# Weight sums of the feed-forward stage made once, during the mLSTM stage, and read back from DRAM

## The chip, the cores and the metric

The kernel runs on one core of one Trainium2 chip. The metric is the device time of one execution in microseconds (us). TensorE (PE) multiplies, VectorE (DVE), ScalarE (ACT) and GpSimd (POOL) work elementwise, SyncE (SP) issues nearly all DMAs. Each engine takes its instructions in the order in which they are written, and waits on semaphores.

## The reference

One layer of a hybrid decoder for a prompt of 2048 tokens and 64 sample tokens. The change touches how the matrix `w_ffn_in` is prepared; the sum itself stays.

```python
h = rms_norm(x, norm_mix_w)
... attention heads and mLSTM heads on h @ w_in ...
x = x + jnp.concatenate([o_att, o_ml], axis=-1) @ w_out
h2 = rms_norm(x, norm_ffn_w)
g, u = jnp.split(h2 @ w_ffn_in, 2, axis=-1)          # w_ffn_in: 1024 x 5632
gp = jnp.concatenate([conv_buf, g], axis=1)
gc = conv_b + gp[:, 0:T] * conv_w[0] + gp[:, 1:T+1] * conv_w[1] + gp[:, 2:T+2] * conv_w[2]
x = x + (jax.nn.silu(gc) * u) @ w_down
```

## The kernel before

All data are float32. To keep precision, each matrix product is made as three: an operand is rounded on ACT (`_hi`), the rest is subtracted on DVE (`_lo`), and PE adds hi times hi, lo times hi and hi times lo.

The stages follow each other: attention (0 to about 300 us), mLSTM (`mlstm`, to about 670 us), then `late`: the output projection with the second norm (the loop over `positions`, to about 890 us), the feed-forward rounds (to about 1930 us) and the down projection in 77 turns (to the end).

**The mLSTM stage** goes through 17 tiles, one each period; tile 14 is the sample tokens. In a period PE projects the next tile (`project(t + 1, g)`, three groups), and does the recurrence of this one in between (`turn`, `scores`, `sums`). POOL does `keep_v` and `weigh_k` at the start of a period and `square_h` near its end, once DVE's `divide` has made h; `rstd_h` and `weigh_h` then alternate with DVE's `norm_out`, `scale_out` and `finish_out`, which stand in DVE's queue ahead of `make_a` of the next tile, for which PE's `sums` waits. SP loads the tile after next (`load_h`), the row of gates (`load_m`), and stores the last output (`store_o`).

**The feed-forward rounds.** There are three groups of columns of h2 (group 0: 512 prompt tokens and the 64 sample tokens; groups 1 and 2: 768 each). Each group goes through 11 rounds, `r = (G, i)`; a round takes 256 columns of the gate half of `w_ffn_in` (unit u = 0) and 256 of the up half (u = 1). The 2 by 2 block product of a unit is made by seven products of half the size, in Strassen's manner (Winograd's form), `PRODUCTS`. With B11, B21 (left half of the columns) and B12, B22 (right half; top and bottom rows) the seven right-hand sides are B11, B21, B22 and the sums T1 = B12 - B11, T2 = B22 - T1, T3 = B22 - B12, T4 = B21 - T2. A product is 4 chunks of 3 matmuls; 14 products, 168 matmuls, make a round. Group 0 adds `sample_down`, 12 matmuls for the sample tokens.

The weights of a unit come in one DMA of 1 MiB (`load_b`, L2551) into `c_raw[u]`. POOL makes the four sums (`sums_b`, L3372 to L3385): T1 in place in `c_raw`, T2 to T4 in `t_raw[u]`. ACT rounds four pieces (`round_b`): q = 0 is B11, B21, q = 1 is T1, B22, q = 2 is T2, q = 3 is T3, T4. DVE subtracts them (`split_b`) in the same order, and PE's products wait on `b_split`. `t_raw` and `t_lo` are the same memory, so a new sum there waits until PE has used the old one (`w_prod(pool, before(r), 7 * u + 6)`). Since every group needs the same weights, the sums are made three times over the kernel.

SP's order in a round r is: `load_b(0, after(r))`, in group 0 `load_d(before(r))`, `store_act(before(r))` (L2558), `load_b(1, after(r))`. `store_act` holds two waits: for POOL's gates (`w_made`, L2565), and for DVE's sums of the last activations (`w_sums`, L2568). `load_b(1, ...)` stands behind both. At a group's last round `load_next_a` follows: seven DMAs of up to 768 KiB bring the left-hand sides of the next group.

POOL's order in a round (`step`, L3420): `sums_b(r, 1)`, the two gates of the round before, `heads`, `tails`, `sums_b(after(r), 0)`.

## Time and profile before

| | us |
|---|---|
| median of 3 runs | 2361.06 (2360.82 to 2361.8) |
| the profiled execution, its own time | 2364.47 |
| its span, first to last instruction | 2362.7 |
| PE busy | 2253.2 (95%) |
| DVE busy | 1620.8 (69%) |
| POOL busy | 1034.6 (44%) |
| ACT busy | 899.3 (38%) |
| DMA moved | 333.95 MB, mean 141 GB/s |

The rounds of the feed-forward stage take some 1040 of the 2363 us. A share of busy time is a mean over stages that differ: the views by stretch and the chain of waits tell which engine a stage waits for. Matmuls overlap in the profile, so their rate is read from the distance of their starts and not from their durations.

### The profile page before, as it was taken

The numbers are of one execution on the slowest core, as the hardware profiler recorded it, in microseconds if no ns is written. First come the engines' busy times: TensorE is split into PE (matmuls) and PEld (weight loads), VectorE is DVE, ScalarE is ACT, GpSimd is POOL, SyncE is SP. The second block draws the span as 40 slices with busy tenths as digits, with TensorE's granted clock in tenths as the row PEclk, the third lists the DMA queues.
The fourth block names the chain that finished last, engine by engine and source line by source line (L and its number), as shares of the span: only waits on it lengthen the run. The fifth ranks groups of instructions, "written<-read, shape, count | busy, mean of one in ns | idle before, by whom it ended". The sixth has DMA issues, their size and how long they took to land.

```text
span 2362.7 us, 34413 instructions
## 1 busy us (share of the span) xinstructions
PE 2253.2 (95%) x13423; PEld 1984.9 (84%) x13423; DVE 1620.8 (69%) x2271; ACT 899.3 (38%) x1524; POOL 1034.6 (44%) x811
## 2 busy tenths in 40 slices
PE   7999999999999998888879999989999999999999
PEld 6899878887777888777768999988999998888887
DVE  5666655556573457888878899888998974445653
ACT  4555622222232324444444444444444433233331
POOL 4333312222121346655554666655666630245730
PEclk9999999999999998999998999999999999999999
DMA  8433222222154553444344333353333345686454
GB/s 283 151 126 121 79 86 81 81 81 67 45 183 142 192 184 122 156 139 138 132 161 140 117 118 116 118 181 100 119 118 119 119 158 190 219 289 202 139 177 165
DMA packets 208076, 333.95 MB, mean 141 GB/s; under 512 B 23083, under 2 KB 148679, under 8 KB 205847
## 3 DMA queue, kind: packets, MB, share of 16 engines
q1 hardware_dynamic: 207883, 331.69, 41.5%
q8 instruction: 107, 1.75, 0.3%
q14 instruction: 54, 0.44, 0.1%
q0 software_dynamic: 32, 0.07, 0.0%
HBM read 235.42 MB, written 97.24 MB: 141 GB/s over the span
## 4 chain that ended last, share of the span: by engine, by line
PE 65%; DVE 7%; DMA 5%; issue 4%; POOL 3%; ACT 3%; SPq 0%; DVEq 0%; POOLq 0%; ACTq 0%
PE bank L114 12%; PE bank L115 12%; PE bank L116 12%; PE bank L2803 9%; PE bank L2804 8%; PE bank L2805 8%; DMA late_c_raw<-in_w_ffn_in_dram 3%; DVE late_t L3184 1%; DVE late_s_act L3154 1%; DVE late_t_lo L3129 1%; POOL late_c_raw L3381 1%; POOL late_t_raw L3385 1%; DVE late_t L3187 1%; DMA late_a_raw<-h_parts 1%; ACT late_t_hi L2930 1%
## 5 line engine op out<-in xcount | busy, mean ns | idle before, releaser
L2803 PE MATMUL bank<-late_a_hi,late_b_hi 128*128 128x384 f32 (+1 forms) x1056 | 350.0, 331 | 56.3 <-issue 18.6
L2804 PE MATMUL bank<-late_a_lo,late_b_hi 128*128 128x384 f32 (+1 forms) x1056 | 344.7, 326 | 0.0
L2805 PE MATMUL bank<-late_a_hi,late_b_lo 128*128 128x384 f32 (+1 forms) x1056 | 343.2, 325 | 0.0
L2803 PE MATMUL bank<-late_a_hi,late_t_hi 128*128 128x384 f32 (+1 forms) x792 | 262.9, 332 | 19.6 <-DVE late_gp L3172 8.5
L2803 PEld LDWEIGHTS bank<-late_a_hi,late_b_hi 128*128 128x128 f32 x1056 | 201.7, 191 | 69.1 <-issue 36.3
L2804 PE MATMUL bank<-late_a_lo,late_t_hi 128*128 128x384 f32 (+1 forms) x792 | 258.3, 326 | 0.0
L2805 PE MATMUL bank<-late_a_hi,late_t_lo 128*128 128x384 f32 (+1 forms) x792 | 257.6, 325 | 0.0
L114 PE MATMUL bank<-late_e_hi,late_y_a_hi 128*128 128x512 f32 x616 | 242.1, 393 | 2.1 <-DVE late_e_lo L3202 2.1
L116 PE MATMUL bank<-late_e_hi,late_y_a_lo 128*128 128x512 f32 x616 | 242.6, 394 | 0.0
L115 PE MATMUL bank<-late_e_lo,late_y_a_hi 128*128 128x512 f32 x616 | 241.7, 392 | 0.0
L3379 POOL TENSOR_TENSOR late_t_raw<-late_c_raw 128x512 f32<-128x512 f32 x64 | 84.2, 1315 | 327.9 <-DMA late_c_raw<-in_w_ffn_in_dram 300.4
L3129 DVE TENSOR_TENSOR late_t_lo<-late_t_raw,late_t_hi 128x512 fp32r<-128x512 f32 (+1 forms) x132 | 220.8, 1672 | 10.0 <-POOL late_t_raw L3385 10.0
L3129 DVE TENSOR_TENSOR late_b_lo<-late_c_raw,late_b_hi 128x1024 fp32r<-128x1024 f32 x128 | 187.3, 1463 | 46.6 <-ACT late_b_hi L2930 46.6
L3200 DVE TENSOR_TENSOR late_y_a_lo<-late_y_a_raw,late_y_a_hi 128x1024 fp32r<-128x1024 f32 x77 | 111.4, 1447 | 154.6 <-ACT late_y_a_hi L2989 154.6
L2804 PEld LDWEIGHTS bank<-late_a_lo,late_b_hi 128*128 128x128 f32 x1056 | 201.9, 191 | 0.0
L2805 PEld LDWEIGHTS bank<-late_a_hi,late_b_lo 128*128 128x128 f32 x1056 | 201.6, 191 | 0.0
L2803 PEld LDWEIGHTS bank<-late_a_hi,late_t_hi 128*128 128x128 f32 x792 | 150.0, 189 | 32.6 <-issue 16.7
L2930 ACT ACTIVATE late_b_hi<-late_c_raw 128x1024 fp32r<-128x1024 f32 x128 | 134.9, 1054 | 94.7 <-POOL late_c_raw L3381 62.1
L3184 DVE SCALAR_TENSOR_TENSOR late_t<-late_gp,late_cc,late_t 128x768 f32<-128x768 f32 (+1 forms) x132 | 163.2, 1237 | 0.4
L114 PE MATMUL bank<-att_next_hi,att_next_hh 128*128 128x512 f32 (+1 forms) x384 | 159.9, 416 | 2.1 <-DVE ml_vx L1941 2.1
L115 PE MATMUL bank<-ahead_ml_w_lo,att_next_hh 128*128 128x512 f32 (+1 forms) x384 | 154.1, 401 | 0.0
L116 PE MATMUL bank<-att_next_hi,att_next_hh 128*128 128x512 f32 (+1 forms) x384 | 153.1, 399 | 0.0
(380 smaller groups left out, 5187.1 us busy)
## 6 DMA issues: line engine op xcount, KB each, us to landing
late_c_raw<-in_w_ffn_in_dram SPq DMA_DIRECT2D x64, 1024.0 KB, 5.1
late_y_a_raw<-act_parts SPq DMA_DIRECT2D x77, 512.0 KB, 3.6
late_e_raw<-in_w_down_dram SPq DMA_DIRECT2D x77, 256.0 KB, 4.1
act_parts<-late_s_act SPq DMA_DIRECT2D x22, 768.0 KB, 4.4
att_next_hh<-h_parts SPq DMA_DIRECT2D x16, 1024.0 KB, 4.8
late_d_raw<-in_w_down_dram SPq DMA_DIRECT2D x11, 1024.0 KB, 7.6
late_a_raw<-h_parts SPq DMA_DIRECT2D x14, 768.0 KB, 12.7
act_parts<-late_t SPq DMA_DIRECT2D x22, 384.0 KB, 2.5
```

The lines of the kernel that those rows point to most:

```text
L114: nc.tensor.matmul(out, a_hi, b_hi, start=first, stop=False)
L115: nc.tensor.matmul(out, a_hi, b_lo, start=False, stop=False)
L116: return nc.tensor.matmul(out, a_lo, b_hi, start=False, stop=last)
L2803: nc.tensor.matmul(out, w_h, hi[:, c, :], start=first, stop=False, skip_group_check=True)
L2804: nc.tensor.matmul(out, w_h, lo[:, c, :], start=False, stop=False, skip_group_check=True)
L2805: ins_ = nc.tensor.matmul(out, w_l, hi[:, c, :], start=False, stop=last, skip_group_check=True)
L2930: nc.scalar.activation(hi, raw, ACT.Copy).then_inc(b_rounded, 1)
L3129: nc.vector.tensor_tensor(lo, raw, hi.bitcast(F32), ALU.subtract).then_inc(b_split, 1)
L3154: nc.vector.tensor_tensor(out, x, y, op).then_inc(act_summed, 1)
L3184: ins_ = nc.vector.scalar_tensor_tensor(tb, gp[:, x, HEAD - s:HEAD - s + G.pn], col, tb, ALU.mult, ALU.add)
L3200: nc.vector.tensor_tensor(y_lo[s][:, :], y_raw[s][:, :], y_hi[s][:, :].bitcast(F32), ALU.subtract).then_inc(y_split, 1)
L3379: nc.gpsimd.tensor_tensor(tt(T3), b(1, 1), b(0, 1), ALU.subtract).then_inc(b_summed, 1)
```

## The change

Four parts.

1. **Sums ahead.** A class `SumsAhead` makes T1 to T4 of all 22 units (11 rounds, two halves) during mLSTM tiles 2 to 12 and puts them into a DRAM tensor `weight_sums`. A tile handles four items; an item is half a unit (two chunks of the top rows and the two of the bottom rows under them). For an item SP loads 2 times 256 KiB, POOL makes 4 subtractions of 128x256 elements, and SP stores 256 + 3 times 128 KiB in four DMAs (B11 and T1 as one image, T3, T4, T2). POOL does them between `weigh_k` and `square_h`, 16 subtractions in a tile. SP stores a tile's items one period later, in pairs, and loads the next into the same buffers as soon as the stores of that item have landed. The buffers lie over memory that is free then. `wait_all` stands on ACT, DVE and POOL ahead of the sample tile and on SP in `late`.
2. **Rounds load them.** `load_b` becomes two DMAs of 512 KiB: B11 and T1 from `weight_sums`, B21 and B22 from `w_ffn_in`. A new `load_t` loads the 768 KiB of T3, T4, T2 into `t_raw[u]` when PE has done the last T product of the unit of the round before. `sums_b` and the waits on it are gone from POOL, ACT and DVE.
3. **SP's order in a round** is now `load_t(1, r)`, `load_b(0, after(r))`, `load_d`, `store_act(before(r))`, `load_b(1, after(r))`, `load_t(0, after(r))`, `store_sums(before(r))`: the store of the activations' sums, with its wait on DVE, has left `store_act`.
4. In the down projection the two semaphores of a turn's two loads become one (`ye_in`), so ACT and POOL wait for both.

```diff
@@ mlstm, SP's period @@
+                for pair in range(2):
+                    if SUM_FROM < t.c <= SUM_TO:
+                        ahead.store(sp, t.c - 1, 2 * pair)
+                        ahead.store(sp, t.c - 1, 2 * pair + 1)
+                    if SUM_FROM <= t.c < SUM_TO:
+                        ahead.load(sp, ins, t.c, 2 * pair)
+                        ahead.load(sp, ins, t.c, 2 * pair + 1)
                 if 1 <= t.c <= samp.c:
                     store_o(sp, t - 1)
...
@@ mlstm, POOL's period @@
                 weigh_k(t)
+                if SUM_FROM <= t.c < SUM_TO:
+                    ahead.make(pool, t.c, 0)
+                    ahead.make(pool, t.c, 1)
+                if is_sample(t):
+                    ahead.wait_all(pool)
                 square_h(pool, t)
...
+    def load(self, sp, ins, slot, n):
+        unit, e = self.item(slot, n)
+        i, u = unit // 2, unit % 2
+        if slot > SUM_FROM:
+            sp.wait_ge(self.moved[n], self.moves(slot))
...
+    def make(self, pool, slot, pair):
+        nc = self.nc
+        two = (2 * pair, 2 * pair + 1)
+        for n in two:
+            pool.wait_ge(self.moved[n], self.moves(slot) + 32)
+            nc.gpsimd.tensor_tensor(self.diff[n], self.low[n][:, :, 1, :], self.top[n][:, :, 1, :], ALU.subtract).then_inc(self.made, 1)
...
+    def store(self, sp, slot, n):
+        unit, e = self.item(slot, n)
+        sp.wait_ge(self.made, self.count(slot, n, 3))
...
@@ late, SP @@
-            sp.dma_start(raw_of(r, u)[:, :].rearrange("p (c n) -> p c n", c=KC), src).then_inc(b_in[u], 16)
+            sp.dma_start(raw_of(r, u)[:, 0:IMAGE], sums_dram[2 * i + u, :, 0:IMAGE]).then_inc(b_in[u], 16)
+            sp.dma_start(raw_of(r, u)[:, IMAGE:2 * IMAGE].rearrange("p (c n) -> p c n", c=KH), src).then_inc(b_in[u], 16)
+
+        def load_t(u, r):
+
+            if r is None:
+                return
+            w_prod(sp, before(r), 7 * u + 5)
+            sp.dma_start(t_raw[u][:, :], sums_dram[2 * r[1] + u, :, IMAGE:IMAGE + 3 * KH * P]).then_inc(t_in[u], 16)
...
                 if r != FIRST:
+                    load_t(1, r)
                     load_b(0, after(r))
...
                     store_act(before(r))
                     load_b(1, after(r))
+                    load_t(0, after(r))
+                    store_sums(before(r))
...
@@ late, ACT's round_b @@
-                act.wait_ge(b_in[u], 16 * (turn(r) + 1))
-            else:
-                w_summed(act, r, 4 * u + q)
+                act.wait_ge(b_in[u], 32 * (turn(r) + 1))
+            elif q == 2:
+                act.wait_ge(t_in[u], 16 * (turn(r) + 1))
...
@@ late, POOL's step @@
             p = before(r)
-            if p is None:
-                heads(r)
-            sums_b(r, 1)
             if p is not None:
                 gate(p, 0)
                 gate(p, 1)
-                heads(r)
+            heads(r)
             tails(r)
-            sums_b(after(r), 0)
```

**Where instructions stand.** POOL in one round of group 0, before. `late_t<-late_t,late_up` are the gates, the copies are `heads` and `tails`, L3379 to L3385 are the sums of one unit.

```order
L3393 TENSOR_TENSOR late_t_7680<-late_t_7680,late_up 128x576 x2
L3398 COPY late_cc<-conv_cols 128x40
L3400 MEMSET late_gp 128x2x2
L3405 COPY late_gs<-late_cc 128x16x2
L3413 COPY late_gs<-late_gp 128x16x8
L3414 COPY late_s_act<-late_gp 128x32
L3417 COPY halo<-late_gp 128x4
L3379 TENSOR_TENSOR late_t_raw<-late_c_raw_7675 128x512
L3381 TENSOR_TENSOR late_c_raw_7675<-late_c_raw_7675 128x4x128
L3383 TENSOR_TENSOR late_t_raw<-late_c_raw_7675 128x512
L3385 TENSOR_TENSOR late_t_raw<-late_c_raw_7675,late_t_raw 128x512
L3379 TENSOR_TENSOR late_t_raw<-late_c_raw_7676 128x512
```

POOL in the same round now:

```order
L3494 TENSOR_TENSOR late_t_8401<-late_t_8401,late_up 128x576 x2
L3499 COPY late_cc<-conv_cols 128x40
L3501 MEMSET late_gp 128x2x2
L3506 COPY late_gs<-late_cc 128x16x2
L3514 COPY late_gs<-late_gp 128x16x8
L3515 COPY late_s_act<-late_gp 128x32
L3518 COPY halo<-late_gp 128x4
```

The eight subtractions of a round are gone; the gates follow the last round's copies at once.

SP in one round of group 0, before, from `load_b(0)` on; `late_c_raw` with its two numbers are the buffers of u = 0 and u = 1, `late_d_raw` is the down weight, and `act_parts` takes activations:

```order
L2551 DMA late_c_raw_7675<-in_w_ffn_in_dram 128x8x256
L2555 DMA late_d_raw<-in_w_down_dram 128x2x1024
L2566 DMA act_parts<-late_t_7679 128x2x256
L2567 DMA act_parts<-late_t_7679 128x256
L2569 DMA act_parts<-late_s_act 128x4x256
L2551 DMA late_c_raw_7676<-in_w_ffn_in_dram 128x8x256
```

SP in one round of group 0 now, from `load_t(1)` on (`weight_sums` is the new tensor):

```order
L2655 DMA late_t_raw<-weight_sums 128x1536
L2647 DMA late_c_raw_8396<-weight_sums 128x1024
L2648 DMA late_c_raw_8396<-in_w_ffn_in_dram 128x4x256
L2659 DMA late_d_raw<-in_w_down_dram 128x2x1024
L2670 DMA act_parts<-late_t_8400 128x2x256
L2671 DMA act_parts<-late_t_8400 128x256
L2647 DMA late_c_raw_8397<-weight_sums 128x1024
L2648 DMA late_c_raw_8397<-in_w_ffn_in_dram 128x4x256
L2655 DMA late_t_raw<-weight_sums 128x1536
L2681 DMA act_parts<-late_s_act 128x4x256
```

The load of the second unit's weights stood behind the store from `late_s_act` (DVE's sums) and now stands ahead of it; two loads of `late_t_raw` are new.

POOL in one mLSTM tile, before (`ml_vx` and `ml_kw` are `keep_v` and `weigh_k`, L1488 is `square_h`):

```order
L2115 TENSOR_TENSOR ml_vx<-att_next_z,ones 128x4x128
L2123 TENSOR_TENSOR ml_kw<-att_next_z,att_next_cols 128x256
L1488 TENSOR_TENSOR ml_hq<-ml_h 128x512
L1494 TENSOR_TENSOR ml_hr<-ml_hvar,mhalf 128x4
L1499 TENSOR_TENSOR ml_hq<-ml_h,ml_norm 128x512
```

POOL in an mLSTM tile now, to the first two of the second pair of items (six more follow ahead of `square_h`); pieces 0, 1 and 3 have buffers of their own, piece 2 uses the memory of `norm_mix` and `mask`:

```order
L2125 TENSOR_TENSOR ml_vx<-att_next_z,ones 128x4x128
L2133 TENSOR_TENSOR ml_kw<-att_next_z,att_next_cols 128x256
L2306 TENSOR_TENSOR ml_piece_diff_4301<-ml_piece0b,ml_piece0a 128x256
L2306 TENSOR_TENSOR ml_piece_diff_4302<-ml_piece1b,ml_piece1a 128x256
L2310 TENSOR_TENSOR ml_piece0a<-ml_piece0a 128x2x128
L2310 TENSOR_TENSOR ml_piece1a<-ml_piece1a 128x2x128
L2314 TENSOR_TENSOR ml_piece0b<-ml_piece0b,ml_piece0a 128x2x128
L2314 TENSOR_TENSOR ml_piece1b<-ml_piece1b,ml_piece1a 128x2x128
L2318 TENSOR_TENSOR ml_piece0b<-ml_piece0b 128x2x128
L2318 TENSOR_TENSOR ml_piece1b<-ml_piece1b 128x2x128
L2306 TENSOR_TENSOR mask<-norm_mix 128x256
L2306 TENSOR_TENSOR ml_piece_diff_4303<-ml_piece3b,ml_piece3a 128x256
```

Sixteen subtractions stand between `weigh_k` and `square_h`.

SP in two mLSTM periods, before:

```order
L1518 DMA att_next_hh<-h_parts 128x2048
L1507 DMA ml_neg_m<-gate_rows 128x512
L1436 DMA mixed<-ml_o 128x512
L1518 DMA att_next_hh<-h_parts 128x2048
L1507 DMA ml_neg_m<-gate_rows 128x512
```

SP in one mLSTM period now, first half: the stores of items 0 and 1 of the tile before, and their loads for this tile:

```order
L1519 DMA att_next_hh<-h_parts 128x2048
L1508 DMA ml_neg_m<-gate_rows 128x512
L2324 DMA weight_sums<-ml_piece0a 128x512
L2326 DMA weight_sums<-ml_piece_diff_4301 128x256
L2328 DMA weight_sums<-ml_piece0b 128x2x128 x2
L2324 DMA weight_sums<-ml_piece1a 128x512
L2326 DMA weight_sums<-ml_piece_diff_4302 128x256
L2328 DMA weight_sums<-ml_piece1b 128x2x128 x2
L2295 DMA ml_piece0a<-in_w_ffn_in_dram 128x2x256
L2295 DMA ml_piece0b<-in_w_ffn_in_dram 128x2x256
L2295 DMA ml_piece1a<-in_w_ffn_in_dram 128x2x256
L2295 DMA ml_piece1b<-in_w_ffn_in_dram 128x2x256
```

A second half of the same kind, for items 2 and 3, follows ahead of the store from `ml_o`: 24 DMAs are added to the three of a period.

## Rows read from the trace of the kernel before

**Rows 1.** Busy time by stretch: mLSTM, group 0's rounds, group 1's rounds; first line: columns.

```profile
core 0: us, PE busy (x) PEld busy (x) DVE busy (x) ACT busy (x) POOL busy (x), PEclk, DMA share, GB/s
...
330.00:600.00 270.00, 270.00 (x1395) 216.36 (x1393) 161.44 (x291) 60.52 (x148) 72.87 (x65) 1.00 0.21 75
...
918.00:1225.00 307.00, 268.68 (x1786) 241.87 (x1787) 255.92 (x326) 137.02 (x190) 186.67 (x159) 0.98 0.38 128
...
1255.00:1572.00 317.00, 315.31 (x1767) 310.41 (x1766) 282.37 (x277) 131.27 (x169) 197.72 (x134) 0.99 0.35 114
```

**Rows 2.** Chain that ended last, one round of group 0: start, us, what.

```profile
1040.97 0.36 SPq L2569
...
1041.38 6.10 DMA late_c_raw<-in_w_ffn_in_dram
...
1047.61 1.35 POOL late_t_raw L3379
...
1049.03 2.17 POOL late_c_raw L3381
...
1057.09 1.32 DVE late_t_lo L3129
...
1068.81 1.05 ACT late_d_hi L2936
...
1071.81 0.36 SPq L2569
```

**Rows 3.** Timeline of PE, group 0: start, us, engine line op names shape.

```profile
1040.33 0.45 PE L114 MATMUL bank<-late_d_hi,late_acts_hi 128*64 128x512 f32 x1
...
1043.98 0.40 PE L2803 MATMUL bank<-late_a_hi,late_b_hi 128*128 128x288 f32 x1 [0.66 <-DVE late_b_lo L3129]
1044.22 0.30 PE L2804 MATMUL bank<-late_a_lo,late_b_hi 128*128 128x288 f32 x1
...
1045.54 0.29 PE L2805 MATMUL bank<-late_a_hi,late_b_lo 128*128 128x288 f32 x1
```

**Rows 4.** DVE by line and form, group 0's rounds: count, busy us, mean ns, idle before.

```profile
L3154 DVE TENSOR_TENSOR late_s_act<-late_t 128x256 f32<-128x256 f32 x19 | 18.2, 960 | 0.0
L3154 DVE TENSOR_TENSOR late_s_act<-late_s_act,late_t 128x256 f32<-128x256 f32 x10 | 13.3, 1328 | 1.0
L3154 DVE TENSOR_TENSOR late_s_act<-late_t,late_s_act 128x256 f32<-128x256 f32 x9 | 3.8, 419 | 0.0
```

**Rows 5.** Change from group 0 to 1: chain, then PE; last line group 1 to 2.

```profile
1227.25 7.70 DMA late_a_raw<-h_parts
...
1238.66 0.66 PE L2803 MATMUL bank<-late_a_hi,late_b_hi 128*128 128x384 f32 x1 [10.15 <-issue]
...
1590.70 0.66 PE L2803 MATMUL bank<-late_a_hi,late_b_hi 128*128 128x384 f32 x1 [8.42 <-issue]
```

**Rows 6.** Timelines of one mLSTM period: POOL, DVE, PE, SP; in brackets idle and releaser.

```profile
442.01 1.04 POOL L1488 TENSOR_TENSOR ml_hq<-ml_h 128x512 f32<-128x512 f32 x1 [12.44 <-DVE ml_h L1450]
...
448.42 1.07 POOL L2123 TENSOR_TENSOR ml_kw<-att_next_z,att_next_cols 128x256 f32<-128x256 f32 x1
...
451.37 0.76 DVE L1919 TENSOR_TENSOR ml_a<-bank,ml_e 128x256 f32<-128x256 f32 x2 [2.35 <-PE bank L1614]
...
457.35 1.06 PE L1626 MATMUL bank<-ml_vx,ml_a 128*128 128x129 f32 x8
...
437.32 0.32 SPq L1518 DMA_DIRECT2D att_next_hh<-h_parts  x1
...
457.54 0.32 SPq L1518 DMA_DIRECT2D att_next_hh<-h_parts  x1
```

**Rows 7.** POOL by line and form, whole span: prices of elementwise operations.

```profile
L2115 POOL TENSOR_TENSOR ml_vx<-att_next_z,ones 128x512 f32<-128x512 f32 x16 | 20.5, 1282 | 34.0 <-DVE ml_vx L1941 30.0 <-PE bank L1630 4.0
...
L1238 POOL TENSOR_TENSOR att_v<-att_z,ones 128x128 f32<-128x128 f32 x16 | 7.4, 460 | 0.0
```

**Rows 8.** DMA queue over 1300 to 1400 us: packets, MB, share of 16 engines.

```profile
q1 hardware_dynamic: 9613, 11.39, 35.5%
```

More of the change, by code:

```diff
@@ L1285, in _, with mlstm @@
             tiles_each(period, 0, NT)
-def mlstm(nc, block, k, C, bank, ins, outs, h_dram, o_dram, start, first):
+def mlstm(nc, block, k, C, bank, ins, outs, h_dram, o_dram, start, first, ahead):
     QM, KM, VM, OM = 0, MLQ, 2 * MLQ, 2 * MLQ + MLV
@@ L1850, in period @@
                 if is_sample(t):
+                    ahead.wait_all(act)
                     forget_s()
@@ L2074, in period @@
                 if is_sample(t):
+                    ahead.wait_all(dve)
                     gates_s()
@@ L2241, in half_tile, with late @@
     return (G.base + h * G.PH) // P + j - G.tiles[0]
-def late(nc, block, k, first, bank, ident, mhalf, ins, outs, o_dram, x1_dram, h2_dram, a_dram, conv_cols, halo, ml_end):
+def late(nc, block, k, first, bank, ident, mhalf, ins, outs, o_dram, x1_dram, h2_dram, a_dram, sums_dram, conv_cols, halo, ml_end, ahead):
     CC = SB * (CW - 1) + CW + 1
@@ L2567, in store_act, with store_sums @@
             sp.dma_start(a_dram[2, i, :, cols], act_part(r, 1, 1)).then_inc(landed, 16)
+        def store_sums(r):
+            if r is None:
+                return
+            G, i = r
+            cols = slice(G.half_col(), G.half_col() + G.PH)
+            landed = act_out[turn(r) % 2]
             w_sums(sp, r, 3)
@@ L2672, in _ @@
             if p.c == SAMPLE_AT + 1:
+                ahead.wait_all(sp)
                 load_b(0, FIRST)
+                load_t(0, FIRST)
             if p is final:
@@ L2678, in _ @@
                 proj.wait(sp, final)
+                load_t(1, FIRST)
                 load_d(FIRST)
@@ L2685, in _ @@
         load_b(1, after(FIRST))
+        load_t(0, after(FIRST))
         for G in groups:
@@ L3550, in trunk_step @@
         with nc.Block() as block:
[L3551 removed]
+            ml_end = mlstm(nc, block, ml_stage, C, bank, ins, outs, h_dram, o_dram, start, first, made_ahead)
             inner.close()
```

116 lines of the change are left out of this document (75 added, 41 removed).

## The prediction

> **What bounds the kernel now.** I read the busy time by stretch first, then the chain of waits inside one feed-forward round, then the timelines of the engines in the places that the change touches.
>
> By stretch [rows 1] three cases stand apart. In the mLSTM stage PE is busy all 270.00 of 270 us: PE bounds it, and POOL works 72.87 of 270 us. In group 1's rounds PE is busy 315.31 of 317 us although DVE is at 282.37: PE bounds these too, and group 2's are of the same shape. Only in group 0's rounds does PE have gaps: 268.68 of 307 us.
>
> The chain of group 0 [rows 2] shows why. It repeats every 1071.81 - 1040.97 = 30.84 us: SP's store of the activation sums (L2569), then the load of the second unit's weights which is queued behind it (6.10 us), then POOL's sums (1.35, 2.17 and two more), ACT, DVE's `late_t_lo`, PE's next unit and DVE's work on it, and at last DVE's activation sums, which release the store again. PE itself needs less: its matmuls start (1045.54 - 1044.22) / 10 = 0.132 us apart [rows 3], 168 of them are 22.2 us; `sample_down` takes 1043.98 - 1040.33 less the wait of 0.66, 3.0 us. That is 25.2 us, 5.6 below the period.
>
> **The change, part by part.** The sum is made against the profiled span of 2362.7 us. The profiled execution took 2364.47, 3.4 more than the median of 2361.06; I take the difference of the sum off the median.
>
> *Group 0's rounds.* Two links of the chain go. `load_b(1)` no longer stands behind the wait on DVE's sums; it waits for DVE's split of the same buffer, about the middle of the round, so it is issued some 12 us earlier (`late_t_lo` at 1057.09 against 1071.81). And POOL's four subtractions between the load and ACT are gone, about 7 us (from 1047.61 to before 1054.8: ACT and DVE follow, DVE at 1057.09) [rows 2]. In their place `late_t_raw` is loaded by `load_t`. Its buffer is free about 1.6 us before the unit's end (one product of 12 matmuls at 0.132); for u = 1 `sample_down` (3.0) passes, and the second T product of the next round is a whole unit (11 us) later. A load of 1 MiB took 6.10 us, this one is 768 KiB: it is hidden with some 7 us to spare. For u = 0 likewise.
>
> DVE gets lighter too. Its second activation sum (`late_s_act<-late_s_act,late_t`, 128x256) takes 1328 ns while POOL makes sums, and the last one, of the same size with POOL idle, 419 ns; the mean of the other two is 960 [rows 4]. These alone are 0.91 + 2 x 0.54 = 2.0 us of a round. The Trainium skill ("SBUF — State Buffer", Who interferes with whom) says the same of the cause: a DVE instruction with two SBUF inputs and a GpSimd instruction that reads SBUF lock each other out for a whole instruction. What it adds here comes with the mLSTM stage.
>
> What is late next: the tail of DVE's queue in a round. The second silu, ACT's `round_d` (1.05 us at 1068.81), DVE's split of it, two activation sums, two taps and three splits stand ahead of PE's second product of the next round; this chain doesn't run over POOL, and PE waited 0.66 us at its head even now [rows 3]. Also POOL's gates now run right where DVE makes those splits, and can cost one blocked instruction. From below the round is 25.2 us plus restarts of a few tenths: 26.0. From above, if a gate blocks one split and each product waits once, 28.0. I take 26.9, nearer to the floor, because PE in group 1 keeps its rate [rows 1] with DVE busy for 89% of the time, and here DVE would have at most (255.92 / 307 x 30.84 - 2.0) = 23.7 of 26.9 us, 88%. The gain is 11 x (30.84 - 26.9) = 43 us; bounds 11 x 2.8 = 31 and 11 x 4.8 = 53.
>
> *Groups 1 and 2.* PE already has no gaps within the rounds, so nothing is gained, and DMA traffic grows from 114 GB/s [rows 1] by 1.5 MiB a round of some 29 us, 54 GB/s, far from full. 0 us; bounds +1 and -3.
>
> *Changes of group.* PE stands still 10.15 us and 8.42 us [rows 5]. The left-hand sides were queued behind `store_act` with DVE's sums and behind the 1 MiB of `load_b(1)`; that load is now out of the way. A MB costs 35.5 us / 11.39 = 3.1 us of the queue [rows 8], and DVE's sums come about 1 us sooner, so both changes shrink by about 4 us: 8 us. The first load took 7.70 us [rows 5], so it can't be much more; bounds 3 and 12.
>
> *The mLSTM stage* pays. The period is 457.54 - 437.32 = 20.2 us. POOL's own work runs from 442.01 to 448.42 + 1.07, 7.5 us, and leaves 12.7 free [rows 6]. A subtraction of 256 elements lies between 460 ns (128) and 1282 ns (512) [rows 7]; on the line between, 0.73 us, plus 0.07 from one to the next (1047.61 + 1.35 to 1049.03) [rows 2]: 16 x 0.80 = 12.9 us. So POOL is full: `square_h` comes at least 0.2 us later in each of 11 tiles, and with about 1 us of blocked instructions 1.2 us, 13 in all. This has slack: DVE idles 2.35 us ahead of `make_a`, and PE's `sums` start at 457.35, 5.2 us after `make_a` has ended [rows 6], 7.6 us together. Beyond that PE waits: some 6 us.
>
> By the lock of the page above, each of DVE's two-input instructions in this stretch (the gate caps, the division) may be held for up to a whole subtraction; with three held in the division the tail would come 2 us later per tile and the stage would lose about 20 us instead. No row of before shows such a pair here.
>
> DMA is nearly full too: 75 GB/s [rows 1] x 20.2 us are 1.5 MB, the new moves 4 x (512 + 640) KiB are 4.7 MB, and 6.2 MB x 3.1 us are 19.3 of 20.2 us [rows 8]. SP waits twice a tile for stores to land before it may load; while it does, the queue still holds the other item's stores, so I expect a rate just below what is needed, and add 3 us. Total -9 us; bounds 0 (the line's price, no conflicts) and -30 (a tile of 23.5 us).
>
> *The rest.* In the down projection a turn's rounding waits for two loads instead of one. PE is fed from a ring of four turns, so 0. The waits ahead of the sample tile are for stores issued a period earlier: 0.
>
> The sum: 43 + 0 + 8 - 9 = 42 us less, a span of 2321; against the median 2361.06 - 42 = 2319 us.
>
> **The rivals.**
>
> *A. Group 0 stays bound by its chain.* DVE's tail, lengthened by POOL's gates, could hold the round at 29 us or more. For it: PE's waits in the round are on DVE. Against it: two links of 6 and 7 us leave the cycle. Gain 11 x 1.8 = 20, plus 5, less 9: 2345.
>
> *B. The mLSTM stage goes over to DMA and POOL.* A tile takes 23.5 us instead of 20.2: 11 x 3.3 = 36, less the slack of 7.6: 29 us lost instead of 9. For it: the two loads on the DMA queue and POOL computed above, both over 95%. Result 2339. It is inside my range.
>
> *C. Slower than before: SP's queue becomes the bound of the mLSTM stage.* 27 DMAs stand in a tile, each about 0.4 us of SP's time (0.32 for `load_h` [rows 6]), 11 us; four times SP waits until a store has landed. At 2 us each this fits (19 us); if stores land after 5 us, since they queue behind 6 MB, a tile is 11 + 4 x 4 = 27 us, `load_h` stands behind it, and PE gets its tile late: 11 x 6.8 - 8 = 67 us lost, against 51 gained: 2377. It decides from 25.3 us a tile.
>
> *D. The change doesn't do what it says:* the T loads land late, because they can't be issued before PE has used the old ones, and group 0 waits for them as it did for the sums, groups 1 and 2 begin to. Against it are the 7 us to spare. About 2360.
>
> **How the numbers follow.** Forecast (rounds of 26 to 28, a stage that loses 0 to 20): 0.68. A 0.11, B 0.10, C 0.07, D 0.04. The forecast alone spans 2361 - 53 - 12 = 2296 to 2361 - 31 - 3 + 20 = 2347; since its ends need all at once, 2302 to 2340. With A and B inside and half of the faster corner, the range is 2298 to 2346, which leaves out C, D and about 0.08 at the edges. What a measurement of this kernel can tell from no change is about 0.2%, 4.7 us. Faster by more: 0.68 + 0.11 + 0.10 = 0.89, less a little for B going further: 0.88. Within: 0.04, most of D. Slower: C and the rest, 0.08.
>
> **What would show it.** Right: rounds of group 0 of 26 to 28 us; `late_s_act` at 0.42 us in all four; ACT's rounding of `late_t_hi` not waiting for DMA; the first load of `late_a_raw` before the end of PE's round, and a PE gap below 7 us there; POOL's idle time in mLSTM near zero in tiles 2 to 12, PE's waits there below 20 us in all. Wrong: ACT waiting for DMA in `late_t_hi` (D); PE idle ahead of L1626 of more than 2 us a tile (B), or ahead of the projection, waiting for `att_next_hh` (C); PE's waits in group 0 on DVE's `late_b_lo` growing (A).

## The result and the profile after

The changed kernel takes 2370.35 us (median of six, 2366.43 to 2372.82), the kernel before 2361.61 beside it: ratio 1.0034, interval 1.0024 to 1.0045. It is slower by 0.34%, where 1.8% faster was forecast. The profiled execution took 2366.69 us, near the low end of the six; before's took 2364.47. One execution of one experiment took 7511 us and is left out of every number below.

Where the 2.2 us between the two profiled executions come from, by the starts of PE's rounds:

| stretch | before | after | difference | forecast |
|---|---|---|---|---|
| to the first feed-forward product | 887.1 | 897.3 | +10.2 | +9 |
| ten rounds of group 0 | 311.3 | 294.2 | -17.0 | -39 (of -43 for eleven) |
| last round before, first after each change of group | 163.6 | 151.9 | -11.7 | -12 (-8, and -4 for the eleventh round of group 0) |
| rounds 2 to 10 of groups 1 and 2, with group 2's last | 569.4 | 589.5 | +20.1 | 0 |
| down projection | 431.3 | 431.9 | +0.6 | 0 |

Forecast and profile lie 44 us apart: 22 of them in group 0's rounds, 20 in those of groups 1 and 2.

Busy time by stretch after, to be read beside [rows 1] (the same columns):

```profile
330.00:600.00 270.00, 262.59 (x1330) 208.55 (x1329) 173.70 (x281) 58.77 (x142) 194.57 (x234) 1.00 0.80 258
918.00:1225.00 307.00, 272.01 (x1853) 252.76 (x1851) 229.08 (x342) 135.01 (x195) 57.95 (x80) 0.98 0.58 191
1255.00:1572.00 317.00, 307.88 (x1728) 301.14 (x1728) 226.68 (x267) 126.89 (x165) 60.07 (x50) 1.00 0.49 163
```

POOL has nearly nothing left to do in the rounds (197.72 to 60.07 us in group 1), DVE is lighter by 56 us there, and yet PE, which had no gaps in group 1, has them now: 307.88 of 317. A lighter DVE and a slower PE together say that something got worse at one place of the round, not in the sum.

That DVE got lighter is as forecast. DVE by form in group 0's rounds (count, busy us, mean ns), against [rows 4]:

```profile
L3245 DVE TENSOR_TENSOR late_b_lo<-late_c_raw,late_b_hi 128x1024 fp32r<-128x1024 f32 x41 | 74.8, 1825 | 2.0 <-ACT late_b_hi L3050 2.0
L3245 DVE TENSOR_TENSOR late_t_lo<-late_t_raw,late_t_hi 128x1024 fp32r<-128x1024 f32 x20 | 24.3, 1213 | 0.0
...
L3270 DVE TENSOR_TENSOR late_s_act<-late_s_act,late_t 128x256 f32<-128x256 f32 x10 | 4.3, 426 | 1.4 <-DVE late_s_act L3270 0.5
```

The second activation sum fell from 1328 to 426 ns. One form went the other way: `late_b_lo`, of the same size as `late_t_lo` (1213 ns, undisturbed), has a mean of 1825. Its instructions are of two kinds, 1.22 and 2.4 to 2.5 us. The timelines of one round of group 0 show which are long (start, us, engine, line, names; in brackets idle time and releaser). PE:

```profile
1043.69 0.40 PE L2923 MATMUL bank<-late_a_hi,late_b_hi 128*128 128x288 f32 x1 [0.39 <-DVE late_b_lo L3245]
...
1072.60 0.40 PE L2923 MATMUL bank<-late_a_hi,late_b_hi 128*128 128x288 f32 x1 [0.39 <-DVE late_b_lo L3245]
...
1076.25 0.40 PE L2923 MATMUL bank<-late_a_hi,late_t_hi 128*128 128x288 f32 x1 [1.79 <-DVE late_t_lo L3245]
```

DVE:

```profile
1071.32 1.22 DVE L3245 TENSOR_TENSOR late_b_lo<-late_c_raw,late_b_hi 128x1024 fp32r<-128x1024 f32 x1
...
1073.10 2.49 DVE L3245 TENSOR_TENSOR late_b_lo<-late_c_raw,late_b_hi 128x1024 fp32r<-128x1024 f32 x1 [0.19 <-ACT late_b_hi L3050]
1075.52 0.68 DVE L3245 TENSOR_TENSOR late_t_lo<-late_t_raw,late_t_hi 128x512 fp32r<-128x512 f32 x1
...
1077.62 2.43 DVE L3245 TENSOR_TENSOR late_b_lo<-late_c_raw,late_b_hi 128x1024 fp32r<-128x1024 f32 x1
```

POOL, the two gates:

```profile
1073.08 1.43 POOL L3494 TENSOR_TENSOR late_t<-late_t,late_up 128x576 f32<-128x576 f32 x1 [15.29 <-DVE late_up L3288]
1076.71 2.26 POOL L3494 TENSOR_TENSOR late_t<-late_t,late_up 128x576 f32<-128x576 f32 x1 [2.19 <-DVE late_up L3288]
```

The round is 28.91 us. The gate starts 0.02 us ahead of DVE's split and takes 1.43; the split takes 2.49, its own 1.22 and another 1.27. Behind the split stands `late_t_lo`, and PE waits 1.79 us for that. In the kernel before POOL's queue had the second unit's sums ahead of the gates, and these waited for a DMA. POOL of the kernel before, in a round of group 1 that begins at 1342.71:

```profile
1345.69 1.29 POOL L3379 TENSOR_TENSOR late_t_raw<-late_c_raw 128x512 f32<-128x512 f32 x1 [10.93 <-DMA late_c_raw<-in_w_ffn_in_dram]
...
1352.79 4.11 POOL L3393 TENSOR_TENSOR late_t<-late_t,late_up 128x768 f32<-128x768 f32 x2
```

The gates (L3393) ran 10 us into the round. There too they met DVE's splits (2.32 us at 1352.87 for a `late_t_lo` that takes 0.68 alone), but PE did not wait. With the sums gone nothing holds the gates back: they start the moment that silu and the combines allow, when DVE makes the splits that PE wants next.

In group 1 the gate is 768 wide, and the same happens. DVE, then POOL, then PE:

```profile
1329.77 2.85 DVE L3245 TENSOR_TENSOR late_b_lo<-late_c_raw,late_b_hi 128x1024 fp32r<-128x1024 f32 x1 [0.26 <-ACT late_b_hi L3050]
...
1334.74 2.85 DVE L3245 TENSOR_TENSOR late_b_lo<-late_c_raw,late_b_hi 128x1024 fp32r<-128x1024 f32 x1
```

```profile
1329.68 1.85 POOL L3494 TENSOR_TENSOR late_t<-late_t,late_up 128x768 f32<-128x768 f32 x1 [14.98 <-DVE late_up L3288]
```

```profile
1330.39 0.34 PE L2923 MATMUL bank<-late_a_hi,late_b_hi 128*128 128x384 f32 x1
...
1333.28 0.44 PE L2923 MATMUL bank<-late_a_hi,late_t_hi 128*128 128x384 f32 x1 [0.59 <-DVE late_t_lo L3245]
...
1361.36 0.34 PE L2923 MATMUL bank<-late_a_hi,late_b_hi 128*128 128x384 f32 x1
```

The gate now starts 0.7 us ahead of PE's first product of the round (1330.39). The third to tenth rounds of group 1 and the second to tenth of group 2 are 30.97 to 31.01 us (29.7 to 30.2 before).

A second wait is new in group 0. From the view of waits (engine, line, what it waited for: us, times, longest us):

```profile
ACT late_d_hi L3056 <- DMA late_d_raw<-in_w_down_dram: 36.9, 9, 5.0
```

Before, this line had 2.6 us in three waits. SP's queue says why (start, us of issue):

```profile
1048.82 0.32 SPq L2647 DMA_DIRECT2D late_c_raw<-weight_sums  x1
1049.18 0.44 SPq L2648 DMA_DIRECT2D late_c_raw<-in_w_ffn_in_dram  x1
1049.66 0.51 SPq L2659 DMA_DIRECT2D late_d_raw<-in_w_down_dram  x1
```

`load_d` stands behind `load_b(0)`, which waits for DVE's fourth split. In the fourth to the ninth round of group 0 the load takes 7.1 to 8.1 us (7.1 to 8.5 before), but it is issued 6.0 us into the round (4.3 before), and ACT comes to it 9.0 to 10.6 us in (11.8 to 11.9 before).

Of the mLSTM stage, the view of waits over 460 to 600 us:

```profile
DVE ml_hss L1465 <- POOL ml_hq L1489: 29.5, 6, 6.0
POOL ml_piece_diff L2306 <- DMA ml_piece3b<-in_w_ffn_in_dram: 15.5, 7, 2.7
```

POOL waits for a piece's load while `square_h`, which DVE wants, stands behind it; the tiles take 20.2 us up to the seventh and 21.2 to 22.5 from there.

### The profile page after: what moved, and what is told of

It is laid out like the page before. It is cut to its first block, busy times and chain, and to the rows that moved or that the text cites. A ratio compares the mean times of both kernels' runs of the same rounds, so it can differ in the third digit from the quotient of the medians.

```text
span 2364.9 us, 34529 instructions
## 1 busy us (share of the span) xinstructions
PE 2247.4 (95%) x13423; PEld 1979.2 (84%) x13423; DVE 1493.7 (63%) x2271; ACT 892.3 (38%) x1524; POOL 736.2 (31%) x723
## 4 chain that ended last, share of the span: by engine, by line
PE 59%; DVE 9%; DMA 7%; ACT 4%; issue 3%; SPq 3%; POOL 2%; DVEq 0%; ACTq 0%; POOLq 0%
PE bank L2923 10%; PE bank L2924 10%; PE bank L2925 10%; PE bank L114 9%; PE bank L116 9%; PE bank L115 9%; DVE late_b_lo L3245 3%; DMA ml_piece3b<-in_w_ffn_in_dram 2%; DMA weight_sums<-ml_piece1b 2%; DMA weight_sums<-ml_piece3b 1%; DVE late_t_lo L3245 1%; SPq L2328 1%; ACT late_b_hi L3050 1%; ACT late_t_hi L3050 1%; DVE late_up L3288 1%
## 5 line engine op out<-in xcount | busy, mean ns | idle before, releaser
L3494 POOL TENSOR_TENSOR late_t<-late_t,late_up 128x768 f32<-128x768 f32 (+1 forms) x66 | 143.3, 2171 | 579.7 <-DVE late_up L3288 579.7
L3245 DVE TENSOR_TENSOR late_b_lo<-late_c_raw,late_b_hi 128x1024 fp32r<-128x1024 f32 x128 | 244.8, 1913 | 7.1 <-ACT late_b_hi L3050 7.1
L3316 DVE TENSOR_TENSOR late_y_a_lo<-late_y_a_raw,late_y_a_hi 128x1024 fp32r<-128x1024 f32 x77 | 102.4, 1329 | 200.4 <-ACT late_y_a_hi L3109 200.4
L3109 ACT ACTIVATE late_y_a_hi<-late_y_a_raw 128x1024 fp32r<-128x1024 f32 x77 | 81.7, 1060 | 237.8 <-DMA late_e_raw<-in_w_down_dram 216.1
L3288 DVE TENSOR_TENSOR late_up<-bank,late_up 128x384 f32<-128x384 f32 (+1 forms) x165 | 85.9, 520 | 122.6 <-PE bank L2925 120.6
L3288 DVE TENSOR_TENSOR late_gp<-bank,late_gp 128x384 f32<-128x384 f32 (+1 forms) x165 | 86.0, 521 | 112.8 <-PE bank L2925 112.7
```

The lines of the kernel that those rows point to most:

```text
L3109: nc.scalar.activation(y_hi[s][:, :], y_raw[s][:, :], ACT.Copy).then_inc(y_rounded, 1)
L3245: nc.vector.tensor_tensor(lo, raw, hi.bitcast(F32), ALU.subtract).then_inc(b_split, 1)
L3288: nc.vector.tensor_tensor(dst, bk, src, ALU.add).then_inc(c_dve, 1)
L3316: nc.vector.tensor_tensor(y_lo[s][:, :], y_raw[s][:, :], y_hi[s][:, :].bitcast(F32), ALU.subtract).then_inc(y_split, 1)
L3494: nc.gpsimd.tensor_tensor(t_of(r)[:, x, 0:G.TG], t_of(r)[:, x, 0:G.TG], up[:, x, 0:G.TG], ALU.mult).then_inc(act_made, 1)
```

## The experiments

Unless a text says otherwise, each is the changed kernel with the edit named. A ratio is to the kernel before, run beside it.

**Gates behind tails** (2351.43 us, 0.9955, interval 0.9938 to 0.9972).

```diff
-                gate(p, 0)
-                gate(p, 1)
             heads(r)
             tails(r)
+                gate(p, 0)
+                gate(p, 1)
```

> The changed kernel, with POOL's order within a feed-forward step changed: heads, tails, and only then the two gates, so that they start some 8 us into the round, as they did in the kernel before, and not together with DVE's splits at its start. Theory 1 (the gates, freed from waiting for the sums, lengthen DVE's late_b_lo from 1.2 to 2.4 to 2.9 us where PE's second product waits for what is queued behind it): late_b_lo back to about 1.3 us in group 0 and 1.5 in groups 1 and 2, the rounds of groups 1 and 2 from 30.97 back to 29.8 us (23 us less), those of group 0 from 29.3 to 27.5 or less (20 us less): 2370 - 43 = 2327 us, at least below 2350. Theory 2 (the rounds are longer because of the added DMA traffic of 1.5 MiB a round, or because the loads of the sums land late): the rounds keep their length, 2370 us. Theory 3 (the loss in the mLSTM stage of 10 us is all there is to mend): 2370 us as well.

Groups 1 and 2 came to 29.49 us a round, PE without a gap: the 23 us of theory 1 and a bit more. Nothing was done to the DMA traffic, so theory 2 falls for these groups. Group 0 did not follow: 30.5 to 30.9 us, from the third on, longer than in the changed kernel. So the whole gained 19 us and stayed above the 2350 expected at most.

**Splits in PE's order** (2366.05, 1.0021, 1.0009 to 1.0032): pieces in the order 0, 2, 3, 1.

> The changed kernel, with ACT's roundings and DVE's splits of a unit's weights in the order in which PE uses them: B11/B21, T2, T3 and T4, T1/B22 in place of B11/B21, T1/B22, T2, T3 and T4. The gates stay where they are. Theory 1: late_b_lo still takes up to 2.4 us (2.85 in groups 1 and 2) beside a gate, but it is no longer ahead of T2, so PE's second product waits no more: groups 1 and 2 back to about 29.8 us (23 us less), group 0 to 27.5 to 28 us (about 15 less): 2332 us, at least below 2350. Theory 2 (DMA traffic or late loads of the sums): T2 would be waited for at the DMA, and sooner in the order than before; 2370 us or more.

A miss. The rounds of groups 1 and 2 went from 30.97 to 30.67 only, group 0's were 28.6 to 31.1. With T2 out of the way, the long `late_b_lo` delays the combine behind it (`late_gp`), and PE waited for that: 24.8 us over ten rounds of group 0. A blocked instruction blocks DVE's queue, whatever stands next in it; to change the order does not take the block away.

**Both** (2347.17, 0.9937, 0.9921 to 0.9954).

> Both edits together: gates after tails, and the splits in PE's order. Theory 1: each edit alone takes away the same wait of PE, so together they give little more than the better one, 2320 to 2330 us; group 0's rounds 26.5 to 27.5 us, against the 25.2 us that PE needs. Theory 2 (DMA): 2370 us.

Groups 1 and 2 at 29.49 again; group 0 stayed at 28.8 to 30.8 from the third round on, against the 26.5 to 27.5 expected.

**The work ahead alone** (2376.81, 1.0061, 1.0044 to 1.0078): nobody reads the stored sums; the rounds are before's, with POOL's sums.

> The sums are loaded, made and stored in the mLSTM stage as in the changed kernel, but nobody reads them: the feed-forward rounds are those of the kernel before, with POOL's sums. This is the price of the mLSTM part alone. By the traces (start of the feed-forward rounds 10.2 us later) 2361.6 + 10 = 2372 us; were the mLSTM part less than that and the rounds the cause of all, 2362 to 2365 us. It says also what the rounds and the down projection of the changed kernel are worth without it: 2370 less this.

The mLSTM part costs 14.8 us against the median of before, and its feed-forward rounds begin at 901.6 us. In the kernels that share this stage's code they begin between 896.7 and 904.3, so the 10.2 of the profiled execution is a low one of its kind. The rounds and the rest of the changed kernel thus gain 6.4 us (2376.8 less 2370.4).

**The down projection's load earlier** (2364.6, 1.0008, 0.9997 to 1.0019).

```diff
                     load_t(1, r)
-                    load_b(0, after(r))
                     if before(r) != FIRST and before(r)[0].sample:
                         load_d(before(r))
+                    load_b(0, after(r))
```

> The changed kernel with one load moved in SP's queue: load_d (1 MiB of the down projection's weights for the sample rows) is issued ahead of load_b(0), which waits for a split some 4 us into the round, and not behind it. The trace of the changed kernel has ACT's late_d_hi waiting 36.9 us for it in nine rounds of group 0, where the kernel before had 2.6. Theory 1a (this wait is a second cause in group 0, but in the changed kernel the wait of PE on late_t_lo, 1.8 us a round, stays): ACT's wait goes, the rounds of group 0 become 1 to 1.5 us shorter, 11 x 1.2 = 13 us, 2357; groups 1 and 2 stay at 30.97. Theory 1b (DVE's tail alone sets the round): no change, 2370. DMA traffic as the cause: no change, since the bytes are the same.

ACT's wait for `late_d_raw` went, but group 0's rounds are 28.9 to 29.4 us, where they were 28.9 to 30.3 and one 31.0, ten of them 3.4 us less in all: between the two theories, nearer to 1b. The median is 5.8 us lower. PE's waits in one round are 0.39, 1.78 and 0.87 us, all on DVE's blocked queue. Without them the round would be 26.0.

**All three** (2350.33, 0.9948, 0.993 to 0.9965).

> Gates after tails, splits in PE's order, and load_d ahead of load_b(0). With the first two edits (2347 us) PE's only long wait left in a round of group 0 is 2.2 to 2.6 us for ACT's late_up, which stands behind late_d_hi, waiting up to 5.3 us for this load; the granted clock falls to 0.94 after it. Theory: without this wait the rounds of group 0 come to 26 to 26.5 us, from 30.5: 10 x 4.2 = 42 us less, 2305; groups 1 and 2 stay at 29.49. If something else holds the rounds at 30 us (DVE, or the store of the sums): 2340 to 2347.

A miss of 45 us. ACT, in one round of group 0:

```profile
1055.24 1.05 ACT L3057 ACTIVATE late_d_hi<-late_d_raw 128x1024 fp32r<-128x1024 f32 x1
1063.10 0.31 ACT L3063 ACTIVATE late_acts_hi<-late_t 128x128 fp32r<-128x128 f32 x1 [6.81 <-POOL late_t L3495]
...
1064.99 0.39 ACT L3077 ACTIVATE late_up<-bank 128x288 f32<-128x288 f32 x1
```

PE in the same round:

```profile
1065.52 0.37 PE L2924 MATMUL bank<-late_a_hi,late_b_hi 128*128 128x288 f32 x1 [2.53 <-ACT late_up L3077]
```

Gates behind tails are too late for group 0: its ACT rounds the sample rows' activations (`late_acts_hi`) in mid-round and waits 6.81 us for the gates; the copies that free PE's banks stand behind it. So the same edit that heals groups 1 and 2, which have no sample rows, makes a new wait in group 0. With the load late, as in the first and third experiments, ACT waited for the load in the same place (39.7 us in the first) and only 22.5 us for the gates, against 65.9 here: the one wait hid most of the other.

**With POOL's subtractions spread in the mLSTM stage** (2345.91, the median of three; 0.9932, 0.9914 to 0.995). No row of it is shown, since its trace is of the execution that is left out.

> The same, and POOL's 16 subtractions of a tile in the mLSTM stage spread out: three of the second pair's eight ahead of square_h, one behind it, one behind rstd_h, three behind weigh_h, where all stood ahead of square_h. In the changed kernel's tiles from the eighth on DVE waits 3.7 to 6 us for POOL's square_h, and the tiles take 21.2 to 22.5 us instead of 20.2. Theory M1 (POOL's order makes these tiles long): DVE's wait for ml_hq goes below 1 us, the tiles come to 20.2 to 20.8, 8 to 10 us less than without the edit. Theory M2 (DMA makes them long: 0.80 to 0.88 of the queue's time, loads landing late for the second pair): the tiles stay at 21.5 or more, 0 to 3 us less.

4.4 us less than without the edit, but the two intervals overlap; whether DVE's wait went is not shown. Taken up again below.

**The kernel before with gates first** (2410.0, 1.0203, 1.0188 to 1.0219).

> The kernel before, without any work ahead, with one change in POOL's step: the two gates stand ahead of the four subtractions for the second unit, not behind them, so they start as soon as silu and the combines are done, as in the changed kernel. If the collision of the gates with DVE's splits costs what the changed kernel shows in groups 1 and 2 (1.15 us a round over the kernel before), they go from 29.8 to 30.5 to 31 us, 14 to 23 us; group 0, whose chain runs over the four subtractions, which now wait for the gates, gets longer by up to 2 us a round: 2362 + 15 to 45 us. If the added DMA traffic was the cause: no change in groups 1 and 2.

The rounds of groups 1 and 2 went to 31.67 us, and the whole lost 49 us, more than expected. But the run doesn't isolate the collision: in group 1 ACT now waits 63.6 us in ten rounds for POOL's sums, which stand behind the gates. It shows only that a round does not bear the gates first, in either kernel.

**Gates behind the fourth split** (2321.79, 0.9829, 0.9799 to 0.9859): one wait more, nothing moved.

```diff
             if p is not None:
+                w_split(pool, r, 3)
                 gate(p, 0)
                 gate(p, 1)
```

> The changed kernel with one wait more on POOL: the two gates stay first in the step, but the first waits until DVE has made the fourth split of the first unit's weights, some 5 us into the round. So they run neither beside the splits that PE waits for at the round's start nor (as behind tails) at +11 us, where ACT's late_acts_hi waits for them. Theory: groups 1 and 2 come to 29.5 us as with gates behind tails (23 to 30 us less); in group 0 PE's wait of 1.8 us on late_t_lo goes, those of ACT on late_d_raw (4 to 5 us) stay and may make PE wait for late_up as it did with gates behind tails: 28.5 to 30.5 us a round; 2335 to 2350. If the moment of the gates didn't matter in group 0, only the load: as with gates behind tails, 2351.

48.6 us below the changed kernel, by one wait of POOL, and better than expected. Groups 1 and 2: 29.49 us. Group 0: 26.7 to 30.3, irregular; ACT waits 41.8 us in nine rounds for `late_d_raw`, and PE 11.1 us for `late_up` behind it.

**The same with the order of splits and the load** (2305.82, 0.9767, 0.9752 to 0.9782).

> The same place of the gates, with the splits in PE's order and load_d ahead of load_b(0). Nothing that ACT needs comes late now: no late_d_raw, no gates. With gates behind tails this kernel had rounds of 30.7 us in group 0: PE waited 2.5 us for ACT's late_up behind late_acts_hi, which waited 6.6 us for the gates, and then ran some 4 us at the lower clock. Theory: 26 to 26.5 us a round (29.04 of the kernel with the load alone, less PE's waits of 0.39, 1.78 and 0.87), 11 x 4.3 = 47 us less than that: 2303. If group 0 is bound by something not yet seen: 2340 or more.

Met: 26.35 to 26.47 us in each of nine rounds of group 0.

**The same with POOL's subtractions spread** (2300.59, 0.9745, 0.9731 to 0.976).

> The same, with POOL's subtractions in the mLSTM stage spread around square_h, rstd_h and weigh_h. If POOL's order makes the mLSTM tiles long, the feed-forward rounds start 8 to 10 us earlier: 2294; if DMA does, 0 to 3 us less: 2300 to 2303.

5 us less, though the two intervals just overlap. The tiles from the eighth on stay at 21.4 to 23.6 us, so in the main it isn't the tiles; the one before the sample tile fell from 31.9 to 28.0.

**Spread alone** (2362.82, 1.0004, 0.9992 to 1.0016).

> The changed kernel with POOL's subtractions in the mLSTM stage spread, and nothing else. 8 to 10 us less than the changed kernel (2361) if POOL's order makes the tiles long, 0 to 3 us (2368) if DMA does; DVE's wait for ml_hq falls from 4 to 6 us a tile to below 1 either way. The feed-forward rounds keep their length.

7.5 us less than the changed kernel, but by neither theory: DVE still waits 34.6 us in seven tiles for `ml_hq`, since POOL now stands at the pieces' loads up to 4.2 us, and the tiles are up to 23.8 us long. Where the 7.5 us come from is not shown: in its profiled execution (2365.76) the feed-forward rounds begin at 898.3 us, no sooner than the changed kernel's 897.3.

**Gates behind the fourth split, and the load** (2307.43, 0.9773, 0.9757 to 0.9789), the splits in their old order.

> The changed kernel with the gates behind the fourth split and load_d ahead of load_b(0); the splits stay in their old order. With the gates' place alone 2322 us, with both other edits 2306. If the load accounts for the 16 us (rounds of group 0 of 27.3 to 30.3 us in the former, irregular, 26.4 in the latter): 2306 to 2309. If the order of the splits does: 2318 to 2322.

The load accounts for nearly all of the 16 us; the order of the splits gives 1.6 us, within the intervals. The ten rounds of group 0 take 294.2 us in the changed kernel, 290.9 with the load alone, 281.9 with the gates alone and 266.8 with both. PE at two starts of a round in group 0, and at two points one round apart in group 1:

```profile
1035.51 0.40 PE L2923 MATMUL bank<-late_a_hi,late_b_hi 128*128 128x288 f32 x1 [0.39 <-DVE late_b_lo L3245]
...
1062.03 0.40 PE L2923 MATMUL bank<-late_a_hi,late_b_hi 128*128 128x288 f32 x1 [0.40 <-DVE late_b_lo L3245]
...
1330.46 0.33 PE L2923 MATMUL bank<-late_a_hi,late_b_hi 128*128 128x384 f32 x1
...
1359.95 0.33 PE L2923 MATMUL bank<-late_a_hi,late_b_hi 128*128 128x384 f32 x1
```

DVE in that round of group 0:

```profile
1036.02 1.23 DVE L3245 TENSOR_TENSOR late_b_lo<-late_c_raw,late_b_hi 128x1024 fp32r<-128x1024 f32 x1 [0.20 <-ACT late_b_hi L3050]
...
1040.77 2.08 DVE L3245 TENSOR_TENSOR late_b_lo<-late_c_raw,late_b_hi 128x1024 fp32r<-128x1024 f32 x1
```

POOL:

```profile
1039.43 4.72 POOL L3494 TENSOR_TENSOR late_t<-late_t,late_up 128x576 f32<-128x576 f32 x2 [17.74 <-DVE late_t_lo L3245]
```

26.52 us, 29.49 us. The gates and the splits still hold each other up (4.72 us for two gates, 2.08 for a split), but these splits belong to the unit after, and nobody waits.

**The second pair a tile later** (2309.11, 0.9778, 0.9764 to 0.9793), on top of the kernel of 2300.59.

> All edits together (2300.6 us), and in the mLSTM stage the second pair's eight subtractions are made at the start of the next tile's period, ahead of the first pair's, so that its loads have some 12 us more to land. The bytes are the same. Theory M1' (what holds the tiles is POOL's queue standing at the wait for a load that lands late, with square_h behind it): DVE's wait for ml_hq goes below 1 us, the tiles from the eighth on come to 20.2 to 20.8, 8 us less: 2292. Theory M2 (the queue's bytes): the tiles stay at 21.5 to 22: 2298 to 2303.

8.5 us worse. The stretch of 460 to 600 us, in [rows 1]'s columns:

```profile
460.00:600.00 140.00, 134.76 (x683) 105.98 (x682) 87.17 (x144) 30.06 (x72) 108.76 (x134) 1.00 0.88 284
```

The queue is as full (0.88), and POOL's wait moved to the first pair's loads. The tiles keep to 20.2 us for two longer than without the edit, but DVE still waits 31.7 us in six tiles for `ml_hq`, and the tile before the sample tile got longer (36.9 us against 28.0), perhaps because the last stores, which the sample tile waits for, come a tile later; that was not tried. M1', which had DVE's wait below 1 us, falls; a small part of it may hold.

**Without the copies of B11** (2296.11, 0.9733, 0.9716 to 0.9749), on top of the kernel of 2300.59.

```diff
-        sp.dma_start(dst[:, 2 * e * 2 * P:2 * (e + 1) * 2 * P], self.top[n]...)
+        sp.dma_start(dst[:, 2 * e * P:2 * (e + 1) * P]..., self.top[n][:, :, 1, :])
```

> All edits together, and the mLSTM stage stores T1 alone (128 KiB) where it stored B11 and T1 side by side (256 KiB); the rounds load B11 from w_ffn_in. That is 0.5 of 4.7 MB less in each of the 11 tiles, 11%, in the same count of transfers. Theory M2 (bytes): the DMA share of that stretch falls from 0.88 to about 0.80, the second pair's loads land sooner and the tiles shrink by half of their excess, 4 to 8 us less: 2294. Theory M1': little, 2299 to 2301. In the rounds a load more per unit (512-byte pieces), which is hidden: group 0 stays at 26.4, groups 1 and 2 at 29.49.

The same stretch of this kernel:

```profile
460.00:600.00 140.00, 138.68 (x716) 108.69 (x715) 92.45 (x141) 31.62 (x77) 113.93 (x138) 1.00 0.86 269
```

PE is busy for 138.68 of 140 us. In the changed kernel it was:

```profile
460.00:600.00 140.00, 132.59 (x664) 102.50 (x663) 89.84 (x147) 30.11 (x71) 110.03 (x135) 1.00 0.89 287
```

Now the tiles stay at 20.2 us up to the twelfth. The first feed-forward product:

```profile
886.99 0.38 PE L2926 MATMUL bank<-late_a_hi,late_b_hi 128*128 128x288 f32 x1
```

That is where the kernel before has it (887.1), and 7.6 us ahead of the kernel without this edit (894.6). Of these, 2.3 us were there before the mLSTM stage had begun its first sums (L1634 at 334.3 against 336.6), so 5.3 are the edit's. The median fell by 4.5 us, though the two intervals overlap. By this pair and the next experiment, the bytes were it in the main (M2). The share fell less than expected (0.86, not 0.80), since the tiles got shorter.

**Both of these** (2299.49, 0.974, 0.9724 to 0.9756).

> Both of these. By M1' alone 2292, by M2 alone 2294; if each holds a part, the tiles come to the 20.2 us of the kernel before: 2290 us, the feed-forward rounds start at 889 to 890 us instead of 895.

A miss: 9 us above the 2290 expected, no gain over the former, and the tile before the sample tile is longer again (37.2 us). But beside the kernel of 2309.11 us, from which it differs by the fewer bytes (and the loads of B11 that go with them) alone, it is 9.6 us faster, and here the intervals do not overlap. The best version is the one with 2296.11 us: 2.7% below the kernel before and 3.1% below the changed kernel.

## Why the prediction was wrong

*What bounds the kernel, and the floor of group 0: right.* The floor of 26.0 us with restarts, and 26.9 taken, stand against 26.35 to 26.52 once the two waits are gone. The links that were to leave the chain did leave it: no wait for T loads (rival D false), `late_s_act` at 0.42 us in all four.

*Group 0's rounds, "What is late next": failed.* It named DVE's tail and said that a gate "can cost one blocked instruction", as an upper bound of 28.0, and took 26.9, near the floor, by DVE's busy share. The gates block two splits a round, 1.27 and 1.2 us, at the one place where PE's next product hangs on DVE's queue: 3.0 us of PE's waits in a round, of which 0.9 remain once the gates are moved, and rounds of 28.9 to 31.0, where 26.5 are had without the collision and the late load. A busy share says nothing of that. It is rival A by its mechanism and nearly by its price (29 us), but A was given 0.11.

*Groups 1 and 2, 0 us, bounds +1 and -3: failed, and the furthest outside its bounds.* The step noted the gates' new place in group 0 and did not carry it to the other groups. "PE already has no gaps" was read as room that can't be lost; but the same instruction, moved from mid-round to the start, costs 1.1 us in each of 17 rounds, and 20 us with the last one. Nor did "nothing is gained" hold: with the gates behind the fourth split the same stretch takes 563.8 us, 5.6 less than before. The move was there to be seen in the diff: it deletes the call of `sums_b` ahead of the gates.

*A load that was costed at nothing.* The prediction listed the loads which the change adds (T), and found them hidden, rightly. It did not ask when `load_d` would land and when ACT would want it. The load is no slower; it is issued 1.7 us later, behind a `load_b(0)` that waits for a split which the gates hold up and that is two issues now, and ACT comes to it some 2 us sooner. Mended alone this gave 5.8 us, since the blocked splits held most rounds anyway; once these were mended it gave 14.4 us (2321.8 against 2307.4).

*Changes of group, 8 us: right in size, 9.6 by PE's standstills.* The first load of `late_a_raw` starts at 1218.08 and takes 5.34 us, against [rows 5]; PE stands still 6.68 us instead of 10.15, and 2.30 instead of 8.42.

*The mLSTM stage, 9 us: mechanism half right, mis-sized.* POOL's subtraction took 0.74 us at the median, where the estimate was 0.73. The measured cost is 14.8 us by the run of it alone. The step put the delay on POOL's fullness; the runs put it on the loads, which land late in a DMA queue busy for 0.89 of the stretch (estimated: 19.3 of 20.2 us a tile), with `square_h` behind POOL's wait. Half a MB less in a tile, 11% of what the change adds, brought the start of the rounds back by 5.3 us and the medians of two pairs of kernels down by 4.5 and 9.6; an order of POOL that lets the second pair land later brought nothing in all. Rival B had this with 29 us.

*The page on the shared port.* In the timeline the split that begins 0.02 us behind the gate lasts 1.27 us longer, the gate that begins inside a split takes 2.26 instead of 1.43: each of them stands while the other has the port. By the Trainium skill ("SBUF — State Buffer", Who interferes with whom), a DVE instruction with two SBUF inputs and a GpSimd instruction that reads SBUF contend for a shared pair of ports, an exclusive lock: the one that issues first keeps it, and the other is blocked. The trace agrees within 0.2 us. The prediction applied this rule to the DVE instructions that the change frees and to the mLSTM stage, where it was not the main cost: with all 16 subtractions in a tile but fewer bytes, the stretch from its first sums to the first feed-forward product is 1.6 us longer than before. The gate that the change moves was given one blocked instruction in group 0, in the upper bound, and none in groups 1 and 2.

So a gain of the forecast's size was there: one wait of POOL brings 40 us over the kernel before (2321.79, against the 2319 predicted), and it was given back by an instruction that no line of the change touches. That the two numbers are so near is luck in part. In the profile of that kernel the way to the first feed-forward product is 15 us longer than before (forecast 9), the ten rounds of group 0 gain 29 (39), the changes of group with the eleventh round 19 (12) and the rest of groups 1 and 2 gains 6 (0).

## What to carry to other kernels

When work is taken off an in-order queue, ask of each instruction that stood behind it when it will run now, and beside what: on this kernel two GpSimd gates ran 10 us earlier, into VectorE's two-input splits, and took back the whole gain. A wait that holds an instruction back until its rival for the port has passed can be worth 2%. An instruction wants a window with two ends, though: too early it blocked the splits, behind tails it held up ScalarE (6.8 us a round), and each wait hid the next: moving one load gave 6 us of its own and 14 us once the gates had their place.
